# Two-layer encoder trunk on one core: the place of the first down-projection weights in the load queue, and the last down product taken tile by tile

## The reference, cut to what matters

```python
def conv_gated_ffn(h, w_up, conv_w, conv_b, w_down):
    u = h @ w_up                                   # 512 x 1024 @ 1024 x 5632
    u = conv_b + sum(u_pad[:, j:j + seq] * conv_w[j] for j in range(3))
    gate, val = jnp.split(u, 2, axis=-1)
    return (jax.nn.silu(gate) * val) @ w_down      # 512 x 2816 @ 2816 x 1024

def rms_norm(x, gain):
    normed = x * lax.rsqrt(jnp.mean(x * x, axis=-1, keepdims=True) + 1e-6)
    return normed * gain

for l in range(2):
    ...
    x = x + conv_gated_ffn(rms_norm(x, ffn_norm[l]), ...)
```

## Time and profile before

| What | Value |
|---|---|
| median of 3 runs | 1856.29 us (1855.97 to 1857.71) |
| the profiled execution's own time | 1855.69 us |
| its span, first to last instruction | 1853.9 us |
| PE busy | 1712.5 us, 92% of the span, 12781 matmuls |
| PE weight loads busy | 1403.1 us, 76% |
| DVE busy | 1039.7 us, 56% |
| ACT busy | 815.3 us, 44% |
| POOL busy | 445.8 us, 24% |
| mean granted TensorE clock | 0.970 of full speed |
| DMA | 212.70 MB, mean 115 GB/s |
| chain that ended last | PE 62%, DVE 10%, DMA 9%, ACT 8%, POOL 7% |

### The profile page before, as it was taken

One profiled execution on the slowest core, in us unless ns is written; L12 is line 12 of the kernel. 1 busy time (PEld: TensorE's weight loads), 2 busy tenths in 40 slices (PEclk: granted clock), 3 DMA queues, 4 the chain that ended last, 5 costly groups with the idle time before them and its releaser, 6 DMA issues.

```text
span 1853.9 us, 29685 instructions
## 1 busy us (share of the span) xinstructions
PE 1712.5 (92%) x12781; PEld 1403.1 (76%) x12781; DVE 1039.7 (56%) x1308; ACT 815.3 (44%) x1233; POOL 445.8 (24%) x403
## 2 busy tenths in 40 slices
PE   7998899999999978997798999999999997999599
PEld 6876788778887867886677886678887785888477
DVE  5487577365344536753575455965344564675256
ACT  4244544545543324532345236865553332453143
POOL 2001223210101741046100220530010472125220
PEclk9999999999999998999899999999999998999799
DMA  7300000154213761564343221013331564355413
GB/s 240 102 24 2 4 4 27 48 182 137 95 59 106 241 218 66 182 227 164 103 159 99 93 79 59 1 36 129 110 113 46 182 227 159 114 194 203 170 58 129
DMA packets 116925, 212.70 MB, mean 115 GB/s; under 512 B 4247, under 2 KB 50938, under 8 KB 116794
## 3 DMA queue, kind: packets, MB, share of 16 engines
q1 hardware_dynamic: 103239, 159.59, 25.4%
q0 software_dynamic: 13264, 51.09, 7.7%
q10 hardware_dynamic: 291, 0.12, 0.0%
HBM read 185.62 MB, written 25.17 MB: 114 GB/s over the span
## 4 chain that ended last, share of the span: by engine, by line
PE 62%; DVE 10%; DMA 9%; ACT 8%; POOL 7%; issue 3%; SPq 0%; DVEq 0%; POOLq 0%; ACTq 0%
PE PS L440 38%; PE PS L544 9%; POOL DW L644 5%; DMA diff_dn<-DW 4%; DMA WRAW<-ffn_w_up 4%; ACT WHI L395 2%; DVE WLO L406 1%; PE PS L1882 1%; PE PS L1851 1%; DVE SS L2185 1%; PE PS L1194 1%; PE PS L920 1%; DVE CG L1988 1%; DVE CG L1985 1%; PE PS L2016 1%
## 5 line engine op out<-in xcount | busy, mean ns | idle before, releaser
L406 DVE TENSOR_TENSOR WLO<-WRAW,WHI 128x2048 fp32r<-128x2048 f32 (+1 forms) x106 | 247.1, 2338 | 382.7 <-ACT WHI L395 382.7
L440 PE MATMUL PS<-HIS,WHI 128*128 128x512 f32 x856 | 338.6, 396 | 75.9 <-DVE CG L1988 72.1
L395 ACT ACTIVATE WHI<-WRAW 128x2048 fp32r<-128x2048 f32 (+1 forms) x107 | 203.8, 1908 | 314.9 <-PE PS L440 175.3
L440 PE MATMUL PS<-LOS,WHI 128*128 128x512 f32 x856 | 336.9, 394 | 0.0
L440 PE MATMUL PS<-HIS,WLO 128*128 128x512 f32 x856 | 336.7, 393 | 0.0
L440 PEld LDWEIGHTS PS<-HIS,WHI 128*128 128x128 f32 x856 | 163.3, 191 | 113.3 <-issue 78.6
L440 PE MATMUL PS<-WHI,HIS 128*128 128x512 f32 x608 | 240.5, 396 | 0.0
L440 PE MATMUL PS<-WLO,HIS 128*128 128x512 f32 x608 | 237.1, 390 | 0.0
L440 PE MATMUL PS<-WHI,LOS 128*128 128x512 f32 x608 | 237.1, 390 | 0.0
L440 PEld LDWEIGHTS PS<-HIS,WLO 128*128 128x128 f32 x856 | 163.0, 190 | 34.5
L440 PEld LDWEIGHTS PS<-LOS,WHI 128*128 128x128 f32 x856 | 163.1, 191 | 33.7 <-issue 0.2
(11 more groups left out here) (325 smaller groups left out, 2844.5 us busy)
## 6 DMA issues: line engine op xcount, KB each, us to landing
WRAW<-ffn_w_up SPq DMA_DIRECT2D x88, 512.0 KB, 5.1
RW<-ffn_w_down POOLq DMA_DIRECT2D x22, 1024.0 KB, 7.1
diff_dn<-DW POOLq DMA_DIRECT2D x22, 1024.0 KB, 5.3
WRAW<-cross_wkv SPq DMA_DIRECT2D x16, 1024.0 KB, 5.0
PW<-diff_dn SPq DMA_DIRECT2D x8, 1536.0 KB, 8.7
WRAW<-diff_w_in SPq DMA_DIRECT2D x12, 1024.0 KB, 5.0
WRAW<-ab_w_in SPq DMA_DIRECT2D x10, 1024.0 KB, 5.6
PW<-diff_dn SPq DMA_DIRECT2D x8, 1280.0 KB, 7.5
```

What stands on the lines that cost most here:

```text
L395: A.e.activation(part(WHI[place(i)], i), part(WRAW[raw_slot[i]], i), ACT.Copy).then_inc(S("w_hi"), 1)
L406: V.e.tensor_tensor(part(WLO[place(i)], i), part(WRAW[raw_slot[i]], i), part(WHI[place(i)], i).bitcast(F32), ALU.subtract).then_inc(S("w_l ...
L440: mm = e.matmul(o, l, r, start=(si == 0 and kk == 0 and q == 0), stop=(si == len(steps) - 1 and kk == nk - 1 and q == 2))
```

## The change

Two things. First, the weights of q = 0 and 1 are now loaded behind the last up slab. Second, q = 6 of every down product is taken token tile by token tile: tile 0 with both pieces of weights, then tile 1; `done` is raised once per tile, both pieces' weight places count as free at 14, and DVE adds each tile alone (`ev` now ends at 8). For `dn01` the squares and the norm's DVE work are placed in and around q = 6 instead of behind it. Banks freed earlier are also named so: banks 4 and 5 at `ev` 7 and 8, banks 6 and 7 at 4.

```diff
                 raw_level.append(None)
                 plan.append(None)
-                used_at[i] = (name, 2 * q + p + 1)
-        shares(name, "g", done=14, ev=7)
+                used_at[i] = (name, 14 if q == 6 else 2 * q + p + 1)
+        shares(name, "g", done=14, ev=8)
         shares(name, "seven", wdif=4 * n, shi=5, slo=5)
         diff[name] = nc.dram_tensor(f"diff_{name}", (4, n, P, 512), F32, kind="Internal").ap()
...
             for _bank in range(2, 8):
                 seven_before[_name, _bank] = before[_bank]
-                before[_bank] = (_name, 6 if _bank < 4 else 7)
+                before[_bank] = (_name, (6, 6, 7, 8, 4, 4)[_bank - 2])
             continue
         _groups = gemms[_name]
...
                         other, m = seven_before[name, b]
                         e.wait_ge(*at(other, "ev", m))
-            for p, (a0, a1) in enumerate(((0, 3), (3, n))):
+
+            pieces = tuple(enumerate(((0, 3), (3, n))))
+            steps = [((t,), pc) for t in range(2) for pc in pieces] if q == 6 else [((0, 1), pc) for pc in pieces]
+            for ts, (p, (a0, a1)) in steps:
                 i = i0 + 2 * q + p
                 if q < 2:
                     e.wait_ge(*at(up, "slo", 2 * a1 - 1 + q))
                 e.wait_ge(S("w_lo"), i + 1)
-                for t in range(2):
+                for t in ts:
                     for m in range(a0, a1):
                         for r, (wt, ht) in enumerate(((WHI, SHI), (WHI, SLO), (WLO, SHI))):
...
                                           wt[place(i)][:, m - a0, :], start=(fresh and m == 0 and r == 0),
                                           stop=(m == n - 1 and r == 2), skip_group_check=not fresh)
-                mm.then_inc(sem(name, "done"), 1)
+                if q < 6 or p == 1:
+                    mm.then_inc(sem(name, "done"), 1)
 
     def seven_operand_act(A, name, q):
...
         V.e.tensor_tensor(x, x, PS[:, bank:bank + 2, :], ALU.add).then_inc(sem(name, "ev"), 1)
 
-    def seven_act(A, name, up):
+    def seven_last_sum_dve(V, name, t):
+
+        V.e.wait_ge(*at(name, "done", 13 + t))
+        V.e.wait_ge(*at(name, "ev", 6))
+        x = X[:, 2 + t, 0:512]
+        V.e.tensor_tensor(x, x, PS[:, 4 + t, :], ALU.add).then_inc(sem(name, "ev"), 1)
+
+    def seven_act(A, name, up, tag=None):
         n, i0 = seven[name][2:]
-        for q in range(7):
+        for q in range(6):
             split_hi(A, i0 + 2 * q + 3)
             if q == 1:
                 A.e.wait_ge(*at(up, "sdif", 4 * n))
-            if 1 <= q < 6:
+            if 1 <= q:
                 seven_operand_act(A, name, q)
             split_hi(A, i0 + 2 * q + 4)
-
-    def seven_dve(V, name):
+        if tag is not None:
+            for t in range(NT):
+                square_half_act(A, name, tag, t, 1, 5)
+        split_hi(A, i0 + 15)
+        if tag is not None:
+            for t in range(NT):
+                square_half_act(A, name, tag, t, 0, max(6, 5 + t))
+        split_hi(A, i0 + 16)
+
+    def seven_dve(V, name, tag=None):
         i0 = seven[name][3]
-        for q in range(7):
+        for q in range(6):
             if q >= 1:
                 seven_sum_dve(V, name, q - 1)
             split_lo(V, i0 + 2 * q + 3)
-            if 1 <= q < 6:
+            if 1 <= q:
                 seven_operand_dve(V, name, q)
             split_lo(V, i0 + 2 * q + 4)
-        seven_sum_dve(V, name, 6)
+        seven_sum_dve(V, name, 5)
+        if tag is not None:
+            for t in range(NT):
+                half_var_dve(V, tag, t)
+            V.wait_mine()
+        split_lo(V, i0 + 15)
+        seven_last_sum_dve(V, name, 0)
+        if tag is not None:
+            for t in range(3):
+                var_tile_dve(V, tag, t)
+            scale_tile_dve(V, tag, 0, XN1)
+        seven_last_sum_dve(V, name, 1)
+        if tag is not None:
+            scale_tile_dve(V, tag, 1, XN1)
+            var_tile_dve(V, tag, 3)
+            for t in range(2, NT):
+                scale_tile_dve(V, tag, t, XN1)
+        split_lo(V, i0 + 16)
 
     def seven_sums_pool(G, up, gi):
...
 
 
-    def square_halves_act(A, name, tag):
-
-        for n, (t, c, done) in enumerate([(t, 1, 5) for t in range(NT)] + [(t, 0, 6 + t // 2) for t in range(NT)]):
-            A.e.wait_ge(*at(name, "ev", done))
-            if n > 0:
-                A.e.wait_ge(*at(tag, "sq", n))
-            o = (0, 12)[c] + t
-            A.e.activation(SQH[:, :], X[:, t, c * 512:c * 512 + 512], ACT.Square, accum_out=SM[:, o:o + 1])\
-                .then_inc(sem(tag, "sq"), 1)
-
-    def norm_halves_dve(V, tag):
-        for t in range(NT):
-            half_var_dve(V, tag, t)
-        V.wait_mine()
-        for t in range(NT):
-            var_tile_dve(V, tag, t)
-            if t >= 1:
-                scale_tile_dve(V, tag, t - 1, XN1)
-        scale_tile_dve(V, tag, NT - 1, XN1)
+    def square_half_act(A, name, tag, t, c, done):
+
+        A.e.wait_ge(*at(name, "ev", done))
+        n = (t if c else NT + t)
+        if n > 0:
+            A.e.wait_ge(*at(tag, "sq", n))
+        o = (0, 12)[c] + t
+        A.e.activation(SQH[:, :], X[:, t, c * 512:c * 512 + 512], ACT.Square, accum_out=SM[:, o:o + 1])\
+            .then_inc(sem(tag, "sq"), 1)
 
     def norm_tiles_pe(T, tag, name, early, xn=XN):
...
         for ks in (range(early, early + 4), range(late, late + 4)):
             if ks[0] == late:
-                e.wait_ge(*at(name, "ev", 7 if name in seven else 2 * NT))
+                e.wait_ge(*at(name, "ev", 8 if name in seven else 2 * NT))
             for t in range(NT - 2):
                 e.wait_ge(*at(tag, "xn", t + 1))
...
             for h in range(2):
                 side(f"up{l}{h}", up_act(A, l, h))
-                seven_act(A, f"dn{l}{h}", f"up{l}{h}")
-            if l == 0:
-                square_halves_act(A, "dn01", "n1")
+                seven_act(A, f"dn{l}{h}", f"up{l}{h}", "n1" if (l, h) == (0, 1) else None)
 
 
...
             for h in range(2):
                 side(f"up{l}{h}", up_dve(V, l, h))
-                seven_dve(V, f"dn{l}{h}")
-            if l == 0:
-                norm_halves_dve(V, "n1")
+                seven_dve(V, f"dn{l}{h}", "n1" if (l, h) == (0, 1) else None)
 
 
...
 
             last = {raw_slot[0]: 0, raw_slot[0] ^ 1: None}
-            first_weights = {gemms[f"up{l}{h}"][4 - h][0][0][0]: f"dn{l}{h}" for l in range(2) for h in range(2)}
+            first_weights = {seven[f"dn{l}{h}"][3] - 1: f"dn{l}{h}" for l in range(2) for h in range(2)}
             for i in range(1, len(plan)):
                 if i == fence:
...
 
             for t, c, done in ((0, 1, 4), (1, 1, 5), (0, 0, 6), (1, 0, 7)):
-                e.wait_ge(*at("dn11", "ev", done))
                 for i in range(2 * t, 2 * t + 2):
+                    e.wait_ge(*at("dn11", "ev", done + (1 if done == 7 and i == 3 else 0)))
                     e.dma_start(out[0, i * P:i * P + P, c * 512:c * 512 + 512], X[:, i, c * 512:c * 512 + 512])\
                         .then_inc(S("rows_in0"), 16)
             e.wait_ge(S("rows_in0"), 32 + 16 * 2 * NT)
```

## The result

The changed kernel took 1769.47 us (median of 4: 1767.12 to 1770.06), beside 1857.0 for the kernel before in the same series (median of 4: 1855.97 to 1860.23): ratio 0.9523, 95% interval 0.9507 to 0.9540. It is 87.5 us faster, and the interval means 85 to 92 us. The forecast was 82.8 us less, 1773.5. The direction and the mechanism came as forecast, but the gain is larger than I gave it. The range was 1769 to 1784. As a time the result lies half a microsecond inside its low end; as a difference, which is what the interval is about, 87.5 stands against the 87.3 at most that this low end meant beside 1856.29, the kernel before as I knew it. The profiled execution took 1770.06 us, with a span of 1768.3.

What follows compares the result with a forecast made beforehand. PE was taken to be held by four up-part stalls from a slab queued behind SP's store wait; 79.5 + 2.5 (norm) + 0.8 (end) = 82.8 off 1855.69, plus 0.6 for the median, gave 1773.5 us, range 1769 to 1784.

Steps and rivals of the forecast that it cites:

- The term of 79.5 us: Four up parts: loading the first down weights behind the last up slab gains 16.8, 15.1, 23.6 and 24.0 us.
- Rival B: Up parts: a different link holds PE, so only norm and end gain, 3.3 us less than now, 1853; 2%.
- D: Before `dk`: the norm is not shorter, DVE's split eats what the squares save, 1776 us; 10%, within the range.
- 1.3 us are lost there: `up00`, banks 0 to 3: emptying takes 9.5 us where PE takes 8.2, so 1.3 us are lost.
- rival A: Up parts: POOL is the next bound, its slower pairs cost 10 to 14 us of the gain, 1783.5 to 1787.5; 8%.
- The cover of the `PW` loads: Up parts: later `PW` loads stay hidden, with 26 us of cover in `up00` and 22 in `up01`.
- Rival C: Up parts: `PW` loads come too late, kernel slower, 1857.5 us at a landing of 44 us; 1%.
- The load lands the full 4.1 later: `up01` and `up11`: fourth slab's load, delayed by q = 6 by tile, costs 0 to 2.0 us each; 0 taken.
- no wait over 5 us: Up parts: a sign of success, ACT has no wait over 5 us for `WRAW` there.
- The norm: From PE's end of `dn01` to `dk`: squares and norm around q = 6 save 2.9, 2.5 taken, bounds 0.5 and 3.5.
- The end: Kernel's end: half-width last sum and one store behind it instead of two save 0.8 us, bounds 0.4 and 1.0.
- The pace: Up parts: 0.2267 us per matmul; each stall costs another 2.5 us of slow start at granted clock 0.50.

Runs made afterwards that it cites:

- the queue's line alone: Kernel before with only the first down weights loaded behind the last up slab, q = 6 and norm unchanged: 1772.50 us, ratio 0.9543.
- the three small edits that followed: Changed kernel with third down piece split inside the last up emptying, POOL's pairs spread 2, 2, 1, 1, and second `dk` slab's low part behind the norm's: 1758.07 us.

## Why the prediction was right, and where it was wrong

**The bound and the mechanism: right.** The slab held behind SP's wait was the stall. One line moved it; the queue's line alone gave all of the up parts' gain, and each of the four stalls came back and went by itself. The term of 79.5 us measured 80.3 in the first pair of profiles and 79.6 over all (in the order of the terms 17.3, 15.1, 23.8 and 24.1 against 16.8, 15.1, 23.6 and 24.0 in the first pair; `up10`'s 15.1 took off 1.2 where the terms of `up00`, 0.2 and 1.3, would have given 14.8, so that its hit is partly luck). The 2.5 us of slow start per stall were needed for that; without them the sum would have been short by 10. Rival B fell with this, and D with the norm below.

**"1.3 us are lost there" in `up00`: right size and place, half of the cause.** I read the 9.5 us between banks 0 and 3 as the pace of the emptying against PE's 8.2, and that is what PE lost bank by bank: 1.6 us with the late bank 0. But it is lost only since bank 0 comes free just as PE arrives. Spreading POOL's pairs left the 9.5 us as they were and freed bank 0 earlier, and 1.5 of the 1.6 were gone. So POOL's release of slab 8's split sets the loss together with the pace. My own number, bank 0 free 0.1 us behind PE's arrival, was computed from that release, and I filed it under rival A only. A's mechanism was there already in the forecast case, at 1.6 us in each of two parts rather than 3.

**The cover of the `PW` loads: right, and in `up00` longer than I gave.** I gave 26 and 22 us; the first split came 31 and 22 us after the first issue. Held back by 18 and 9.5 us they cost nothing; held back until 1.2 us was left they cost 13.7 us in all. Rival C lay far off.

**"The load lands the full 4.1 later", bounds 0 and 2.0, 0 taken: right.** `up01` and `up11` took 108.80, which is 480 x 0.2267 to within 0.02. The fourth slab was not later at all: its split began 11.1 and 11.2 us after the start of `up01` and `up11`, where it had been 11.3 and 11.2. ACT still waited for it, 7.1 us for `WRAW` in `up11`, so my sign "no wait over 5 us" failed; before it was 7.7 and 7.3, and PE lost nothing by it in either kernel. One thing did get slower, as forecast, without harm: two subtractions of POOL beside the new DVE work in `up01` took 6.04 us, where the same two took 3.97 before. POOL in `up01`, changed kernel:

```profile
846.08 6.04 POOL L680 TENSOR_TENSOR DW<-RW 128x512 f32<-128x512 f32 x2 [0.56 <-DMA diff_dn<-DW]
852.07 2.67 POOL L680 TENSOR_TENSOR DW<-RW,DW 128x512 f32<-128x512 f32 x2
```

What the change added to these two is 2.1 us, as much as I had allowed. But beside a quiet row the loss is 3.4, more than the 2.1 that I took for the size of it, and that row stood in the kernel before too, in `up00`: 6.08 us for two subtractions at 654.56. The Trainium skill's rule on the shared SBUF interface (GPSIMD Engine Reference, Specifications) agrees with the direction of these rows.

**The norm: a mis-sized term.** Taken 2.5 (2.9 computed), measured 3.4 in the pair of profiles and 3.1 at equal clock. The path was as written: the last scaling ended 4.6 us after PE's end (forecast 4.9), the low parts began at 6.7 (7.2), `dk` at 7.6 (8.1). It came to the 2.9 by steps each a few tenths too long, and I then cut it to 2.5 for nothing in the trace. What I did not see is that q = 6 by tile, which I priced at 0, costs 2.7 us in the norm if the norm is not drawn ahead; it was 0 only because both were in the change.

**The end: a mis-sized term.** Taken 0.8, at most 1.0; measured 1.2. The last sum took 0.69 against 1.22, and one store's issue 0.33 against 0.81 for two: 0.53 and 0.48. The sum's own numbers made 1.0, and I took less. What the other 0.2 are, the rows don't show.

**The step that failed: a term that isn't there.** In "The pace" I counted what the half clock costs behind the four stalls, and stopped. The earlier trace rows are all of `up` parts; I never asked at what clock PE ran behind its other waits, the 2.37 us at the start of `dn01` and `dn11` among them. There 3.2 us lay in the profile before, and the bounds of my range had no room for them. That the first profile after has none of them is partly luck (10 gaps of 20 had it without a stall in the same part). By the stages, leaving out the start and this clock, the change is worth 79.6 + 3.1 + 0.3 (the transposes' clock) + 1.2 = 84.2 us. The clock adds 0 to 3.2, 1.2 by the counts above, which makes 85.4; the medians of the two series, 87.5 and 87.8 less, have 85.4 and 84.3 as the lower ends of their intervals. So 1.4 of the missing 4.7 us are small terms that were all a little too low, most of it norm and end, and some 3.3 are this clock and scatter together. 0.7 of those are no more than the median of before, 1857.0 with a fourth run where I had counted from 1856.29. How much of the rest is clock and how much scatter is not settled, and whether the change makes the half clock rarer is not shown.

**The range.** Its low end took 2.7 for the banks, 1.0 for the norm and 0.2 for the end, and 0.6 for the scatter of the runs, taken from three runs that lay within 1.7 us. The banks gave none of their 2.7, the norm 0.6 to 0.9 of its 1.0, the end 0.4 where 0.2 were allowed. The 0.2 us by which 87.5 exceeds 87.3 are far less than the interval of 85 to 92, so whether the true difference lies in the range is open; that it is above the 82.8 is not. The start alone, which this change doesn't touch, spreads over some 10 us between profiles. A wider allowance for that and for the clock behind the `dn` waits would have held the result.

## What to carry to other kernels

Look past the engine that PE waits for to the queue position of the transfer behind it: SP's wait cost what the next urgent entry behind it cost, and moving it behind the last urgent one took 80 us off without adding or removing an instruction. When the long stalls go, price again what stood in their shadow (POOL's 1.6 us twice, the four short waits of `dn`): the three small edits that followed were worth another 10 us by the stages, 11.7 by the medians. Parts of a change that touch the same end of a stage are to be priced together; q = 6 by tile lost 2.7 us alone and gained 1.3 beside the norm drawn ahead.

## What the runs showed of the hardware that I had not expected

A wait of PE of the same length, 2.37 us, at the same place of the same kernel, was followed by about 3.4 us at 0.50 in one execution and by none in another (`dn01` of the changed kernel: 50.39 and 52.02 us). Over all profiles it was 17 gaps of 28. The 1.01-us waits in `dn00` and `dn10` were never followed by it. The Trainium skill (TensorE: Matmul & The Clock Gate, The HAM clock gate) says that the number of slow matmuls at a kernel's start varies from run to run; these rows show the same in the middle of one. So one pair of profiles can differ by 3 us here, and by up to 10 with the start, without any edit to the code there.
